# A hybrid decoder step on one core: the values of a page quad taken in the step of the next quad's scores

## What is computed

```python
s = einsum(qg, cmp_kv[:, :, 0]) - slopes * d_c
p_cmp = masked_softmax(s, d_c >= 0)
o_cmp = einsum(p_cmp, cmp_kv[:, :, 1])
...
_, idx = lax.top_k(score, 16)
sel = fetch(idx)
s = einsum(qg, ksel) - slopes * d_s
o_slc = einsum(masked_softmax(s, d_s >= 0), vsel)
...
s = einsum(qg, win_kv[:, :, 0]) - slopes * d_w
o_win = einsum(masked_softmax(s, mask_w), win_kv[:, :, 1])
o = g[:, :, 0] * o_cmp + g[:, :, 1] * o_slc + g[:, :, 2] * o_win
```

## Time and profile before

| | us |
|---|---|
| three runs | 1758.44, 1759.17, 1761.16 |
| the profiled execution | 1755.95 |
| its span | 1754.3 |
| attention, 505 to 840 us of the span | 335.0 |
| PE busy in it | 315.45 |
| DVE, ACT, POOL busy in it | 238.11, 218.89, 146.11 |
| granted TensorE clock in it | 0.99 |

### The profile page before, as it was taken

One profiled execution on the slowest core, in us unless ns is written; L12 is line 12 of the kernel. 1 busy time (PEld: TensorE's weight loads), 2 busy tenths in 40 slices (PEclk: granted clock), 3 DMA queues, 4 the chain that ended last, 5 costly groups with the idle time before them and its releaser, 6 DMA issues.

```text
span 1754.3 us, 35862 instructions
## 1 busy us (share of the span) xinstructions
PE 1706.9 (97%) x13523; PEld 1584.2 (90%) x13523; DVE 1211.5 (69%) x1805; ACT 801.9 (46%) x1462; POOL 836.7 (48%) x862
## 2 busy tenths in 40 slices
PE   8999999999989999999999999999999999999998
PEld 7999998999966666667998999999999999999998
DVE  6789965879777677767548754455596979745435
ACT  5311325565876666667325333333433333315335
POOL 2202965555524343444454656665664545326521
PEclk9999999999999999999999999999999999999999
DMA  5323346655533443442414323332584643341114
GB/s 163 123 64 81 88 149 163 187 155 145 137 98 96 145 123 115 128 135 60 148 49 153 111 98 108 111 111 99 178 263 144 180 146 120 103 128 55 49 37 147
DMA packets 179723, 214.61 MB, mean 122 GB/s; under 512 B 22940, under 2 KB 150664, under 8 KB 174799
## 3 DMA queue, kind: packets, MB, share of 16 engines
q1 hardware_dynamic: 174333, 196.30, 36.4%
q0 software_dynamic: 4032, 13.40, 2.6%
q10 hardware_dynamic: 1186, 2.63, 0.5%
HBM read 181.30 MB, written 35.59 MB: 124 GB/s over the span
## 4 chain that ended last, share of the span: by engine, by line
PE 51%; DVE 9%; issue 3%; ACT 3%; DMA 2%; POOL 2%; SPq 1%; ACTq 0%; DVEq 0%; POOLq 0%
PE ps L2825 11%; PE ps L3208 6%; PE ps L2830 5%; PE ps L2583 5%; PE ps L201 3%; PE ps L3213 3%; PE ps L1984 3%; PE ps L1997 3%; PE ps L1970 3%; PE ps L3721 2%; DVE S L2238 2%; PE ps L2024 2%; POOL S L1924 2%; PE ps L207 2%; SPq L3083 1%
## 5 line engine op out<-in xcount | busy, mean ns | idle before, releaser
L1924 POOL TENSOR_SCALAR S<-S,inv,gate_p 128x640 f32<-128x640 f32 (+7 forms) x186 | 124.2, 684 | 187.3 <-DVE inv L2248 187.3
L1311 DVE SCALAR_TENSOR_TENSOR y<-u,conv_w,y 128x1024 f32<-128x1024 f32 x120 | 156.0, 1346 | 1.2
L3208 PE MATMUL ps<-dn_op_hi,dn_hi 128*128 128x264 f32 x672 | 136.8, 285 | 3.8 <-DVE dn_op_lo L3256 3.8
L3208 PE MATMUL ps<-dn_op_lo,dn_hi 128*128 128x264 f32 x672 | 135.7, 283 | 0.0
L659 POOL COPY relaid<-raw 128x512 f32<-128x512 f32 x128 | 83.5, 683 | 87.5 <-PE ps_p L1083 39.3
L2121 ACT ACTIVATE S<-S,mn 128x64 f32<-128x64 f32 (+8 forms) x180 | 108.7, 609 | 1.2 <-DVE mn L2238 1.2
L3139 POOL TENSOR_TENSOR dn_lo<-dn_t_sum,dn_hi 128x512 fp32r<-128x512 f32 x48 | 77.2, 1610 | 65.9 <-ACT dn_hi L3161 65.7
L3208 PEld LDWEIGHTS ps<-dn_op_hi,dn_hi 128*128 128x128 f32 x672 | 103.7, 188 | 5.3 <-DVE dn_op_lo L3256 5.1
L1012 PE MATMUL ps_p<-Ahi,win_hi 128*128 128x352 f32 x456 | 104.1, 328 | 1.5 <-DVE Alo L1288 1.5
L2825 PE MATMUL ps<-s_hi,up_hi 128*128 128x264 f32 x512 | 104.1, 285 | 0.0
L3208 PEld LDWEIGHTS ps<-dn_op_lo,dn_hi 128*128 128x128 f32 x672 | 103.9, 188 | 0.0
(11 more groups left out here) (494 smaller groups left out, 5052.1 us busy)
## 6 DMA issues: line engine op xcount, KB each, us to landing
s_raw<-in_cache_slc_kv_dram SPq DMA_DIRECT2D x256, 128.0 KB, 2.1
raw<-in_cache_cmp_kv_dram SPq DMA_DIRECT2D x188, 128.0 KB, 3.7
dn_op_raw<-hidden SPq DMA_DIRECT2D x21, 1056.0 KB, 6.5
hidden<-cs SPq DMA_DIRECT2D x32, 528.0 KB, 2.6
up_raw<-in_w_up_dram SPq DMA_DIRECT2D x16, 1024.0 KB, 5.4
dn_w<-in_w_down_dram SPq DMA_DIRECT2D x48, 256.0 KB, 4.9
win_raw<-in_w_in_dram SPq DMA_DIRECT2D x38, 256.0 KB, 3.3
raw<-in_cache_cmp_kv_dram POOLq DMA_DIRECT2D x64, 128.0 KB, 3.7
```

The lines of the kernel that those rows point to most:

```text
L1311: i = V_.scalar_tensor_tensor(out=y, in0=x, scalar=w, in1=y, op0=ALU.mult, op1=ALU.add)
L1924: nc.gpsimd.tensor_scalar(x, x, inv[:, n % 3, 3 * e + br:3 * e + br + 1], c.gate_p[:, i, H * br + h:H * br + h + 1], ALU.mult, ALU.mult).t ...
L3208: nc.tensor.matmul(ps[:, 2 * m + j, 0:HC], w_hi[q % 4][:, k, :], x[:, k, HC * j:HC * j + HC], start=(k == 0 and x is op_hi[n]), stop=False)
```

## The change

Three things are written differently. The step of a quad's weights and values comes from a table, the join of the nine quads counts from that table, and the three places that name the join's step follow.

```diff
     START = [FIRST_QUAD + (LAST_QUAD - FIRST_QUAD) * z // (NZ - 1) for z in range(NZ)]
+    WEIGH = [START[z + 1] + 1 for z in range(NZ - 1)] + [START[NZ - 1] + 3]
...
     def weighed_at(st):
 
-        return next((z for z in range(NZ) if START[z] + (4 if place(z) == 0 else 3) == st), None)
+        return next((z for z in range(NZ) if WEIGH[z] == st), None)
...
-    def joined_at(st, after_start):
-        return next((gr for gr in range(2) if START[NQ + (NQ + 1) * gr] + after_start == st), None)
+    def joined_at(st, after_weighing):
+        return next((gr for gr in range(2) if WEIGH[NQ + (NQ + 1) * gr] + after_weighing == st), None)
...
-        gr = joined_at(st, 5)
+        gr = joined_at(st, 2)
...
-                gr = joined_at(st, 6)
+                gr = joined_at(st, 3)
```

## The result

| | us |
|---|---|
| kernel before, median of 20 runs | 1757.51 (1754.65 to 1761.16) |
| changed kernel, median of 20 runs | 1760.17 (1758.3 to 1763.26) |
| ratio | 1.0018, 95% interval 1.0012 to 1.0024 |
| profiled execution of the changed kernel | 1761.49, its span 1759.8 |

The change costs 0.18%, 2.1 to 4.2 us by the interval. The forecast was a gain of 1.3 us, too small to be told from none. The time lies in the range, but partly by luck: the forecast stood on a median of three runs that was 1.7 us above the median of twenty. Against that, 1756.2 was forecast and 1760.2 came, so the working of the prediction is 4.0 us short.

A forecast was written before the change was run, and what follows sets the result against it. PE was taken to bound the kernel (busy 315.45 of the attention's 335.0 us). Terms -1.9 - 1.4 + 0.7 + 1.3 = -1.3 us took 1759.17 to 1757.9 us, a forecast of no difference; range 1752.0 to 1764.0.

The forecast's parts named there:

- Waits that go: PE's value products: their two waits for ACT's copy of the turned weights should go, -1.9 us.
- Waits that shrink: Three PE waits for ACT's copy of mixA, three steps after a start: PE arrives 0.48 later, -1.4 us.
- As work on PE that is zero: The 1.54 us of turn and products per quad only change steps on PE, so their work counts as zero.
- A wait that grows: Two steps after a start, `add_values` (0.35 us) precedes DVE's reciprocal, so POOL starts later at two waits: +0.7 us.
- Banks: Step one after a start: up to five turns in a row on three PE banks; nothing charged.
- Pages: Slots for a quad's second half are freed later, so PE waits for pages: +1.3 us, bounds 0 and 7.1.
- chain of SP's rows: SP's time from products' end to a landed page half: 8.72 us, or 9.63 with the slower issue.
- floor of 1748: PE's listed waits add up to 11.2 us, the most the change can free: 1759.2 - 11.2 = 1748.
- The knot: Faster rival: waits after a quad's start all come free (products, mixA, POOL), 6.4 us, giving 1752.8; chance 0.25.
- the pages were not late: Slower rival: slots refilled too late, PE stands at a quad's second half, 1763.7 us or more; chance 0.15.
- crowded by `add_values`: Slower rival: `add_values` ahead of DVE's copy delays turns in all 17 quads, 6 us in sum, 1763.2; chance 0.06.
- hardly anything: Rival: PE's work is the same and its waits merely change places; counted within the forecast, which had 0.54.

The follow-up runs named there:

- act_order: The changed kernel with the exponentials ahead of the copies of prompt turns in ACT's order of a step; median 1758.34 us, 1.0009 to the kernel before.
- window_moved: The kernel before with only window quads 0 and 9 moved to the step of the next quad's scores; median 1760.01 us, ratio 1.0012.
- page_quads: The changed kernel with window quads 0 and 9 put back and the first join one step earlier; median 1756.02 us, 0.9996 to the kernel before.
- pages_late: The kernel before with only SP's page loads waiting until about when the changed kernel's products would end; median 1758.39 us, ratio 1.0009.
- two_quads: The kernel before with only quads 6 and 11, which waited for ACT's copy, weighed one step later; median 1755.6 us, ratio 0.9991.

## Why the prediction was wrong

- **"Waits that go", -1.9: right.** The line of the products for ACT's copy is gone.
- **"Waits that shrink", -1.4: a step that failed, in sign.** The line rose by 1.9 instead. The waits of the list rose by 3.7 us where the sum had -1.3, and 3.3 of these 5.0 are here. The step let PE come 0.48 later (measured 0.67 at quad 2, where the products have one more row) against an ACT that stood still. ACT did not: its exponentials stand behind the copy of a prompt turn, and that turn behind the products, and its copy of mixA came 1.09 later. Behind quads 2, 4 and 7 this made 1.3 of the 1.9, and act_order, which undoes the order, took 1.4 back. The other 0.6 are behind quad 12 and by its rows belong to the next step; no run tested that one alone.
- **"As work on PE that is zero": failed too, and it is the step that turned the change into a loss.** The amount is the same, but in the places that it left it had filled waits. The list of before cannot show these, since they were filled. Steps 8, 9 and 46 show them now (0.63, 0.80, and 1.28 instead of 0.22, together +2.5 us). window_moved has 1.0012 with only these two quads moved, and page_quads, which puts them back and the join a step earlier, has 0.9996 with mixA still at 4.2.
- **"A wait that grows", POOL +0.7: the sum was near (+1.3), the places were not.** The two waits named are gone. The new ones stand where products left, at step 25 for one, and at step 47.
- **"Banks", 0: about right.** A turn's wait for DVE's copy (L2253) of 0.72 us came at one place, and waits of 0.33 and 0.31 for such copies and 0.90 for ACT's went.
- **"Pages", +1.3: too high in the change, near without the mixA waits.** 0.5 us in the change, 0.2 in pages_late, towards the lower bound of 0; and the quads were 14 and 8, not 3. PE came later to the halves than the subtraction of 1.54 us had it, because its other waits grew. Where act_order took the mixA waits down, pages cost 1.6 us, at quads 3 and 4 as priced and at 14, so the chain of SP's rows was near.
- **The rivals.** The knot did not loosen, the pages were not late, and the step was not crowded by `add_values` in all quads. The slower case that came, filled waits laid bare, was named "hardly anything" and held to be within the forecast. The floor of 1748 holds for what a change can free; I gave no such bound for what a change can lay bare.

## What to carry to other kernels

On the engine that sets the end, moved work is not free: at the place that it leaves, look at what the other engines finish behind it, and charge the idle time that it had covered, which no list of waits shows. When work is put ahead of an instruction, follow each in-order queue behind that instruction before taking the waiting engine as fixed. Try first to move only the pieces that wait, as two_quads does; its gain, 1.4 us by the medians, is too small to be told from none.

## What the hardware showed that was not expected

The place of one copy of 0.6 us in ACT's queue, ahead of or behind the exponentials, was worth 1.0015 in the kernel before, where five waits grew by 0.48 each (0.57 to 1.05 behind quad 2, 0.96 to 1.44 at quad 6).

DVE's lateness in step 46, which the moved work had covered, has a part that no row of PE shows. In the kernel before an instruction of DVE on 128x1 numbers took 1.14 us and ended within 0.02 us of the end of POOL's bias for a later quad:

```profile
686.55 1.14 DVE L2300 TENSOR_TENSOR s_wt<-s_lsum,gate_s 128x1 f32<-128x1 f32 x1
686.63 1.04 POOL L1914 TENSOR_TENSOR s_S<-s_D,s_selb 128x512 f32<-128x512 f32 x1
```

In window_moved the same instruction (L2301 there) took 1.15, and in the changed kernel one of its kind just ahead of it (L2299) 1.25, both again up to the end of POOL's. In page_quads DVE was copying out the join for most of that time; there L2299 took 0.34 and L2301 0.16. No run moved POOL's instruction alone, so what this is worth to PE was not measured.

And the granted TensorE clock differed between executions at places where the work was the same: from 505 to 515 us it was 0.83 before and 0.66 after, though nothing had moved there, and from 605 to 615 us it was 0.83 in the changed kernel and 1.00 in act_order, which shows POOL waits of the same kind there (0.38 and 0.63 us). What lets it fall in one execution and not in another was not settled.
